# A two-layer transformer on one Trainium2 core: the output gate of gated linear attention laid out by token, key norms from a diagonal, and the rotary products moved ahead of a weight unit

## Time and profile before

| What | Value |
|---|---|
| Median of 3 executions | 888.12 us |
| The profiled execution: its own time | 888.98 us |
| The profiled execution: span from the first to the last instruction | 887.2 us |
| Mean granted TensorE clock | 0.997 of full |
| PE busy | 873.5 us, 98% of the span |
| DVE busy | 587.6 us, 66% |
| ACT busy | 441.6 us, 50% |
| POOL busy | 52.8 us, 6% |
| HBM read | 148.67 MB |

### The profile page before, as it was taken

How to read it: one execution, slowest core, us unless ns; L and a number is a source line. 1 busy time by engine, 2 the same in 40 slices (tenths; PEclk the granted TensorE clock), 3 DMA queues, 4 the chain that set the end, 5 groups by cost and what they waited for, 6 DMA issues and landing times.

```text
span 887.2 us, 13796 instructions
## 1 busy us (share of the span) xinstructions
PE 873.5 (98%) x5624; PEld 761.0 (86%) x5624; DVE 587.6 (66%) x898; ACT 441.6 (50%) x644; POOL 52.8 (6%) x80
## 2 busy tenths in 40 slices
PE   8999999999999999999999999999999999999997
PEld 7888999898999888888889999877888888888885
DVE  5785665565646756565686897966477677777544
ACT  6654444654355535444475662547354655555442
POOL 1000000000020100000020015200000100000000
PEclk9999999999999999999999999999999999999999
DMA  9757744445445545455738683412455555565541
GB/s 296 237 190 211 237 144 143 143 146 187 142 141 192 191 147 184 144 202 201 273 115 278 145 177 110 144 49 49 143 190 185 185 177 189 190 190 190 166 166 48
DMA packets 127813, 151.68 MB, mean 171 GB/s; under 512 B 16983, under 2 KB 93142, under 8 KB 127750
## 3 DMA queue, kind: packets, MB, share of 16 engines
q1 hardware_dynamic: 127466, 150.44, 53.1%
q10 hardware_dynamic: 220, 0.28, 0.1%
q0 software_dynamic: 64, 0.07, 0.0%
HBM read 148.67 MB, written 3.68 MB: 172 GB/s over the span
## 4 chain that ended last, share of the span: by engine, by line
PE 86%; DVE 8%; ACT 2%; issue 1%; SPq 1%; DMA 1%; POOL 0%; POOLq 0%; ACTq 0%; DVEq 0%
PE bank L523 18%; PE bank L525 17%; PE bank L524 17%; PE bank L1360 9%; PE bank L549 5%; PE bank L1361 5%; PE bank L550 3%; DVE w_lo L2146 2%; DVE arena L2558 1%; PE bank L1018 1%; PE bank L752 1%; PE bank L732 1%; DMA ring<-in_w_in 1%; PE bank L851 1%; SPq L1441 1%
## 5 line engine op out<-in xcount | busy, mean ns | idle before, releaser
L2146 DVE TENSOR_TENSOR w_lo<-ring,w_hi 128x2048 fp32r<-128x2048 f32 (+1 forms) x134 | 298.3, 2230 | 124.9 <-ACT w_hi L1567 124.5
L1567 ACT ACTIVATE w_hi<-ring 128x2048 fp32r<-128x2048 f32 (+1 forms) x134 | 248.9, 1860 | 97.8 <-PE bank L525 71.8
L523 PE MATMUL bank<-h_both,w_hi 128*128 128x256 f32 x488 | 140.4, 288 | 1.0 <-DVE w_lo L2146 1.0
L525 PE MATMUL bank<-h_both,w_lo 128*128 128x256 f32 x488 | 138.1, 283 | 0.0
L524 PE MATMUL bank<-h_both,w_hi 128*128 128x256 f32 x488 | 138.1, 283 | 0.0
L1360 PE MATMUL bank<-h_both,w_hi 128*128 128x512 f32 x352 | 124.8, 400 | 0.2 <-issue 0.2
L1361 PE MATMUL bank<-h_both,w_lo 128*128 128x256 f32 x352 | 98.8, 281 | 0.0
L523 PEld LDWEIGHTS bank<-h_both,w_hi 128*128 128x128 f32 x488 | 93.5, 192 | 3.1 <-DVE w_lo L2146 1.4
L524 PEld LDWEIGHTS bank<-h_both,w_hi 128*128 128x128 f32 x488 | 93.6, 192 | 0.1
L525 PEld LDWEIGHTS bank<-h_both,w_lo 128*128 128x128 f32 x488 | 93.6, 192 | 0.0
L1360 PEld LDWEIGHTS bank<-h_both,w_hi 128*128 128x128 f32 x352 | 66.1, 188 | 16.7 <-issue 0.5
(11 more groups left out here) (389 smaller groups left out, 1558.5 us busy)
## 6 DMA issues: line engine op xcount, KB each, us to landing
ring<-in_w_in SPq DMA_DIRECT2D x59, 1024.0 KB, 4.9
ring<-in_w_gate_up SPq DMA_DIRECT2D x44, 512.0 KB, 4.7
ring<-in_w_down SPq DMA_DIRECT2D x10, 1024.0 KB, 5.0
ring<-in_w_mem_kv SPq DMA_DIRECT2D x8, 1024.0 KB, 8.6
ring<-in_w_gla_out SPq DMA_DIRECT2D x4, 1024.0 KB, 4.9
ring<-in_w_x_out SPq DMA_DIRECT2D x4, 1024.0 KB, 5.2
ring<-in_w_dsa_out SPq DMA_DIRECT2D x4, 1024.0 KB, 5.2
ring<-in_w_o SPq DMA_DIRECT2D x4, 1024.0 KB, 4.9
```

The lines of the kernel that those rows point to most:

```text
L523: mm(o, ah, bh, start=start, stop=False, skip_group_check=True)
L525: return mm(o, al, bh, start=False, stop=stop, skip_group_check=True)
L1567: act(w_hi[:, k % NHI, at:m], ring[:, order.index(name) % NSLOT, at:m], ACT.Copy)\
L2146: tt_(w_lo[:, i, at:m], ring[:, i, at:m], w_hi[:, k % NHI, at:m].bitcast(F), ALU.subtract)\
```

## The change

In GLA the gate is projected by token, as two wide stripes instead of four channel units, and is multiplied into `g_out` while that is still by token. The transposed result then needs the gain alone: ACT writes `y_hi` straight from the transposes' bank, DVE `y_lo` from the bank and `y_hi`, and branch 0 waits for the banks' reader instead of `y0_split`.

In the second layer the keys' sums of squares are read from the diagonal of the key products by DVE (a product with the identity and a sum along the row), `ss` keeps the queries' 8 products, POOL's power is done in two parts, `r0` goes ahead of `nq0`, `r1` behind it, `sh0` and `sh1` go ahead of `vsvw`, and `nq1` goes behind `vsvw`. DVE's and ACT's programs are reordered to match. Units are then split in the order `kcks`, `kwvc`, `nq0`, `vsvw`, `nq1`, `z0`, `z1`.

The diff, cut to its core:

```
-        units_of("zg", w1, W1_OFF["gz"], 4)
+        wide_units("zg", w1, W1_OFF["gz"], 2)
...
-            project_channels("zg0", h_parts)
-            project_channels("zg1", h_parts)
+            wide_tokens("zg0", h_parts)
...
-            project_channels("zg2", h_parts)
-            project_channels("zg3", h_parts)
+            wide_tokens("zg1", h_parts)
...
-                pe.wait_ge(signal(f"y{b}_split"), n)
+                pe.wait_ge(*(read("yt3") if b == 0 else (signal(f"y{b}_split"), n)))
...
             head_products("kg", 4)
+            pe.wait_ge(*read("kcks"))
+            rope_turn("r0", 0, 2)
             project_channels("nq0", h_parts)
-            pe.wait_ge(signal("squares"), 4)
+            pe.wait_ge(*read("kwvc"))
+            rope_turn("r1", 2, 1)
+            head_products("qg", 0)
+            pe.wait_ge(signal("squares"), 2)
             bank = open_bank("ss")
             for t in range(TT):
-                for i in range(8):
-                    at = 8 * t + i
+                for i in range(4):
+                    at = 4 * t + i
...
-            head_products("qg", 0)
-            pe.wait_ge(*read("kwvc"))
-            rope_turn("r0", 0, 2)
-            rope_turn("r1", 2, 1)
-            project_channels("nq1", h_parts)
-            head_transposes("kk", 4)
-            pe.wait_ge(*read("nq0"))
-            rope_turn("r2", 4, 2)
-            pe.wait_ge(signal("silu_done"), 6)
-            head_transposes("vt", 8)
-            pe.wait_ge(*read("nq1"))
-            rope_turn("r3", 6, 2)
             pe.wait_ge(signal("rope_done"), 1)
             for kv, tile in ((0, 0), (1, 3)):
                 bank = open_bank(f"sh{kv}")
...
             project_tokens("vsvw", h_parts)
+            head_transposes("kk", 4)
+            pe.wait_ge(*read("nq0"))
+            rope_turn("r2", 4, 2)
+            project_channels("nq1", h_parts)
+            pe.wait_ge(signal("silu_done"), 6)
+            head_transposes("vt", 8)
+            pe.wait_ge(*read("nq1"))
+            rope_turn("r3", 6, 2)
...
+            for h in range(H1):
+                sc.wait_ge(*full(f"yt{h}"))
+                for c in range(2):
+                    ins = act(y_hi[0][:, 2 * h + c, :], bank_of(f"yt{h}")[:, 256 * c:256 * c + 256], ACT.Copy,
+                              scale=g_gla_half[:, c:c + 1])
+                ins.then_inc(signal("y0_high"), 1)
...
-            for j in range(4):
-                sc.wait_ge(*read(f"yt{j}"))
-                branch_high(0, j, zg)
...
-            square_of(2)
-            square_of(3)
-            copy("kwvc", pair(ns, 1))
             sc.wait_ge(signal("d_min"), 1)
             act(nA, nA, ACT.Exp, scale=-1.0).then_inc(signal("d_exp"), 1)
             act(qkT, qkT, ACT.Exp).then_inc(signal("d_exp"), 1)
+            copy("kwvc", pair(ns, 1))
             copy("nq0", pair(ns, 2))
             copy("nq1", pair(ns, 3))
             copy_tokens("vsvw", v_tok)
...
             rope_cos("r0", 0, 2)
+            gp.wait_ge(signal("key_sums"), 1)
+            norms(4)
             rope_cos("r1", 2, 1)
-            rope_cos("r2", 4, 2)
...
             level_mask(0)
             level_mask(1)
+            rope_cos("r2", 4, 2)
+            gp.wait_ge(*read("ss"))
+            norms(0)
             rope_cos("r3", 6, 2)
...
-                    ins = tsc(g_out[:, t, 256 * h:256 * h + 256], bank_of(f"og{h}")[:, 256 * t:256 * t + 256],
-                              rstd[:, 8 + 2 * h + t:9 + 2 * h + t], None, ALU.mult)
+                    ins = stt(g_out[:, t, s], bank_of(f"og{h}")[:, 256 * t:256 * t + 256],
+                              rstd[:, 8 + 2 * h + t:9 + 2 * h + t], zg_tok[:, t, s], ALU.mult, ALU.mult)
...
-                    ins = stt(zg[:, 2 * h + c, :], bank_of(f"yt{h}")[:, 256 * c:256 * c + 256], g_gla_half[:, c:c + 1],
-                              zg[:, 2 * h + c, :], ALU.mult, ALU.mult)
+                    ins = stt(y_lo[0][:, 2 * h + c, :], bank_of(f"yt{h}")[:, 256 * c:256 * c + 256], g_gla_half[:, c:c + 1],
+                              y_hi[0][:, 2 * h + c, :].bitcast(F), ALU.mult, ALU.subtract)
...
             lows(splits_by["kg1"] + 2)
+            own = const("id64").unsqueeze(1).broadcast_to([128, 4, CH])
+            for t in range(TT):
+                bank_ready(f"kg{t}")
+                step(tt_(zst[:, 4 * t:4 * t + 4, :], by_chunk(f"kg{t}"), own, ALU.mult))
+                step(nc.vector.reduce_sum(a_cols[:, t, 4:8], zst[:, 4 * t:4 * t + 4, :], X))
+            tsc(a_cols[:, :, 4:8], a_cols[:, :, 4:8], 4 * EPS, None, ALU.add).then_inc(signal("key_sums"), 1)
```

More of the change, by code:

```diff
@@ L1505, in stepper @@
             return step
-        tanh_users = [f"zx{j}" for j in range(4)] + [f"zg{j}" for j in range(4)] + [f"zd{j}" for j in range(4)]
+        tanh_users = [f"zx{j}" for j in range(4)] + [f"zg{c}{t}" for c in range(2) for t in range(TT)] + [f"zd{j}" for j in range(4)]
         tanh_users += [f"bo{b}{c}{t}" for kind, b, c in merge_slots if kind == "bo" for t in range(TT)]
@@ L1718, in _ @@
                 copy(f"kt{j}", kt_tok[:, 4 * j:4 * j + 4, :].rearrange("p a b -> p (a b)"))
-            for j in range(4):
-                bank_tanh(f"zg{j}")
+            for c, t in itertools.product(range(2), range(TT)):
+                bank_tanh(f"zg{c}{t}")
             for h in range(H1):
@@ L1734, in branch_high @@
                 act(pair(y_hi[b], j), pair(src, j), ACT.Copy).then_inc(signal(f"y{b}_high"), 1)
+            for h in range(H1):
[4 more added lines that the diff above has]
+                ins.then_inc(signal("y0_high"), 1)
+            highs(splits_by["zd3"] + 2)
             for j in range(4):
@@ L1738, in _ @@
                 branch_high(2, j, zx)
-            highs(splits_by["zd3"] + 2)
-            for j in range(4):
-                sc.wait_ge(*read(f"yt{j}"))
-                branch_high(0, j, zg)
             def causal_exp(pre, i):
@@ L2361, in _ @@
                     ve.wait_ge(*read(f"kv{c}{j}"))
-            twice_silu("zg2", pair(zg, 2))
-            twice_silu("zg3", pair(zg, 3))
+            for t in range(TT):
+                twice_silu(f"zg1{t}", zg_tok[:, t, 512:1024])
+            ve.wait_ge(*read("zg11"))
             for h in range(H1):
@@ L2372, in _ @@
                 twice_silu(f"zd{j}", pair(zd, j))
+            ve.wait_ge(*read("og3"))
             for h in range(H1):
-                bank_ready(f"yt{h}")
+                lows(splits_by[f"yt{h}"] + 2)
+                ve.wait_ge(signal("y0_high"), h + 1)
                 for c in range(2):
-                    ins = stt(zg[:, 2 * h + c, :], bank_of(f"yt{h}")[:, 256 * c:256 * c + 256], g_gla_half[:, c:c + 1],
-                              zg[:, 2 * h + c, :], ALU.mult, ALU.mult)
+                    ins = stt(y_lo[0][:, 2 * h + c, :], bank_of(f"yt{h}")[:, 256 * c:256 * c + 256], g_gla_half[:, c:c + 1],
+                              y_hi[0][:, 2 * h + c, :].bitcast(F), ALU.mult, ALU.subtract)
                 ins.then_inc(reader(f"yt{h}"), 1)
@@ L2408, in _ @@
             lows(splits_by["zd3"] + 2)
-            for b, src in ((2, zx), (0, zg)):
-                for j in range(4):
-                    low_of_pair(b, j, src)
+            for j in range(4):
+                low_of_pair(2, j, zx)
             lows(splits_by["zd3"] + 3)
@@ L2591, in rope_add, with shifted_blocks @@
                 tt_(ns[:, a:a + n, :], ns[:, a:a + n, :], tmp, ALU.add).then_inc(signal("rope_done"), 1)
-            lows(splits_by["kg1"] + 2)
+            def shifted_blocks():
+                for kv in range(2):
+                    bank_ready(f"sh{kv}")
+                    for g in range(2):
+                        for q in range(2):
+                            r = slice(64 * q, 64 * q + 64)
+                            t_ = bank_of(f"sh{kv}")[r, 256 * g:256 * g + 256].rearrange("p (n s) -> p s n", s=16)
+                            dst = cblk[kv][r, :, 15 * g:15 * g + 15]
+                            for half in range(2):
+                                ins = tt_(dst[:, 8 * half:8 * half + 8, :], t_[:, q::2, half:half + 15],
+                                          cmp_pos[kv][r, 8 * half:8 * half + 8].unsqueeze(2).broadcast_to([64, 8, 15]), ALU.add)
+                    ins.then_inc(reader(f"sh{kv}"), 1)
+            lows(splits_by["kg1"] + 2)
+            own = const("id64").unsqueeze(1).broadcast_to([128, 4, CH])
+            for t in range(TT):
+                bank_ready(f"kg{t}")
+                step(tt_(zst[:, 4 * t:4 * t + 4, :], by_chunk(f"kg{t}"), own, ALU.mult))
+                step(nc.vector.reduce_sum(a_cols[:, t, 4:8], zst[:, 4 * t:4 * t + 4, :], X))
+            tsc(a_cols[:, :, 4:8], a_cols[:, :, 4:8], 4 * EPS, None, ALU.add).then_inc(signal("key_sums"), 1)
             ve.wait_ge(signal("d_exp"), 2)
             for t in range(TT):
-                bank_ready(f"kg{t}")
                 s = slice(4 * t, 4 * t + 4)
```

(13 more changed lines are left out.)

14 lines of the change are left out of this document (8 added, 6 removed).

## The result

The changed kernel takes 890.85 us (median of 10 runs, 889.93 to 891.32); beside it the kernel before took 888.11 us (10 runs, 887.94 to 888.48). The ratio is 1.0027, 95% interval 1.0019 to 1.0034: 2.7 us slower, outside the predicted range and on the other side of no change. The profiled execution took 890.92 us with a span of 889.1.

The account below looks back on a forecast made before the run. PE, busy 98% of the span, was taken as the bound, with a DVE chain nearly equal in the second layer. -1.24 (GLA) + 0.12 (`level(1)`) = -1.12 us took the median from 888.12 to 887.0 us, range 886.0 to 889.8.

Parts of the forecast that it names:

- GLA: Gate projection: two wide stripes replace four channel units, saving PE 1.24 us.
- The edits costed at nothing: In GLA, DVE's scaling of `og` and branch 0's direct reads of `yt`: covered by PE's work, 0 us.
- Second layer, PE's work: Half of `ss` goes, -1.83 us; the stage would end 2.53 us sooner if PE never waited.
- The new last wait: Ahead of `level(1)`: DVE must subtract `z1` before its chain to the transpose; `level(1)` starts 0.12 us later.
- A pause: PE idle 2.8 us ahead of `level(1)`; half clock behind it would cost 1.5 us at most, 0.75 as estimate.
- the clock's fall: Half clock behind the pause ahead of `level(1)`: chance 0.14 with `z1` on time, 0.10 with it late.
- a late load: `z1`'s load taking 6.7 us, not 4.9: `level(1)` +1.92 us, total 888.8; chance 0.20 without half clock.
- The argument against a fall: Second layer: PE has other products, `r3` and `hid`, between its two pauses, which spoke against half clock.
- Rival 2: The pause ahead of `level(1)` halves the clock, `z1` on time: +0.75 us, 887.8 us; chance 0.14.
- Rival 2 together with a late `level(1)`: Half clock and `z1` landing late, so the pause grows: 889.5 to 890.3 us, chance 0.10.
- The rule of the Trainium skill that the prediction weighed: At the pause ahead of `level(1)`: waits between matmul groups slow the clock; by it the time is Rival 2's.

Follow-up runs that it names:

- e1: The GLA part of the diff alone on the kernel before, second layer unchanged: 887.17 us, ratio 0.9987.
- e7: The changed kernel with the values' unit `vsvw` moved back behind the last rotary turn `r3`: 884.82 us, ratio 0.9962.
- e3: The changed kernel with DVE's and ACT's split of `z1` held back behind the triangular start, as before the change: 890.46 us, ratio 1.0024.
- e10: e3 with POOL's masking of the query products also held until the rotary sums are done: 889.10 us, ratio 1.0006.
- e2: The second layer's part of the diff alone on the kernel before, gate unchanged: 892.80 us, ratio 1.0051.
- e8: e1 with five more DVE additions ahead of the transpose that `level(1)` waits for: 893.90 us, ratio 1.0063.
- e4: The changed kernel with four identity products inside `level(1)`, behind PE's wait for the rotary sums: 890.87 us, ratio 1.0032.
- e6: The changed kernel with two identity products straight behind `hid`, ahead of the wait for the rotary sums: 888.23 us, ratio 1.0003.
- e5: The changed kernel with four identity products straight behind `hid`, ahead of the wait for the rotary sums: 888.35 us, ratio 1.0001.

## Why the prediction was wrong

**GLA: right.** -1.24 us forecast; by the trace the two pairs gained 0.58 and 0.55 us on the same pairs of the kernel before (11.68 and 11.61), 1.13 in all, and e1 measured -1.07. The edits costed at nothing cost nothing.

**Second layer, PE's work: right.** `ss` at 1.89 us, and 2.53 us to be had where PE never waits; e7 has 2.54.

**The new last wait: the mechanism right, its size short.** DVE stops for `z1`, and the transpose is what `level(1)` waits for, as forecast. On the old clock (1.55 us added) `level(1)` came at 561.12, forecast 560.12: +1.12 us for the stage where I had +0.12. The load took 5.3 us and not 4.9 from an issue 0.2 us later, which made ACT start 0.7 us late; the sums took 1.74 us from start to start and not 1.40, beside POOL's products. What I took for the cause, though, was only half of it: e3 shows that without `z1` `level(1)` comes only 0.18 us sooner, and e10 that POOL's masking beside the second sum took 1.1 us of the rest.

**The step that failed is "A pause".** I wrote "Three microseconds at half speed delay PE by 1.5 us at most ... I take 0.75", and gave the clock's fall 0.24 of the chances, 0.10 of it with a late load. In its place the runs showed half clock from about 560.3 (0.65 as the mean of a microsecond) to 567.1, 6.8 us, and a cost of 2.39 us in the changed kernel and 2.63 to 2.95 in e2, e3, e8 and e10. The bound was wrong because it carried the length of the slow stretch near the start over to another place. Windows of the kernel before give that stretch its ends:

```profile
7.00:8.00 1.00, 0.55 (x4) 0.55 (x5) 0.50 (x2) 0.71 (x3) 0.73 (x2) 0.90 1.08 383
...
11.00:12.00 1.00, 1.00 (x9) 1.00 (x9) 1.00 (x4) 1.00 (x2) 0.00 (x0) 0.89 1.05 329
```

It ran from about 7.8 to 11.2 us, 3.4 us, so three microseconds was near the truth there, and 1.5 us would have been near it in e4, where the stretch lasted 3.4 us as well and the filler lost 1.7. In the changed kernel it lasted twice as long. What makes it 3.4 us in one place and 6.8 in another no run shows. The argument against a fall, that `r3` and `hid` lie between two pauses, was beside the point: one pause is enough, in either order of the work (e8). The sum with the measured terms: -1.13 + 1.12 + 2.39 = +2.4 us, against +2.7 measured; the rest of 0.3 us isn't accounted for. Rival 2 together with a late `level(1)` was the case that came, and its 889.5 to 890.3 stopped short for the same reason.

The rule of the Trainium skill that the prediction weighed ("TensorE: Matmul & The Clock Gate", "HAM oscillation — how this bites in real kernels": waits between groups of matmuls send the engine back to its slow clock) held here in the traces of the change and of e2, e3, e4, e8 and e10, whose waits were 2.08 us and more, and not in that of e6, with 1.44 us. By that section the next group then starts cold; in the change `level(1)` began at full clock, and the fall came 0.7 us later.

## What to carry to other kernels

Where a reordering leaves PE idle ahead of a dense stage, price the idle time and the clock behind it as two terms. Follow a slow stretch to where the clock comes back, and don't take its length from one place alone: it was 3.4 us near the start and in e4, and 6.8 in five other traces. Before moving a unit of matmuls ahead of a chain on another engine, ask what PE does while that chain runs: the unit was the chain's cover, and left behind the chain's start it turned a loss of 2.7 us into a gain of 3.5. A wait found by name (`z1`) need not be the wait that counts: with it taken away, the next delay in the same chain left a gain of 0.2 us.

## What the runs showed of the hardware

The clock fell behind waits of 2.08 (e4), 2.24 (e10), 3.40, 3.58, 3.86 and 3.90 us, in e4 only when PE had been at work again for over a microsecond, in e2, e8 and e10 already during the wait; behind 1.44 us (e6) it held in the profiled run. It stayed at half for 6.8 us in the change, e2, e3, e8 and e10, which cost 2.39 to 2.95 us, and for 3.4 us in e4, which cost the filler 1.7. Four identity products in the wait, straight behind `hid`, kept it at full speed, and `level(1)` began no later for them (e5).

DVE's sums of 128x512 with both operands in SBUF (`arena`) took 2.69 us for two beside POOL's products of the same shape, and 1.62 with one of those held back; the second sum alone went from 1.75 to 0.68.

One oddity isn't explained. e4's stages lost 3.8 us by its trace (4.95 in the second layer, less 1.13 for the gate), its time only 2.6. In the feed-forward stage its pairs of products (L1360 and L1361 of the kernel before) follow one another every 0.347 us, in every other trace here every 0.353; between `level(2)` and PE's last product that makes 2.0 us. None of these runs was made to find out what sets this pitch.
